# Expert blocks of a mixture layer: slots cut in quarters of 32, 21 units of work in place of 25, six weight tiles loaded ahead

## What is computed

```python
def _hier_moe(m, w_group, b_group, w_expert, b_expert, w_gate, w_up, w_down):
    ...
    g_w, g_idx = lax.top_k(g_prob, 1)              # one group of 4
    e_w, e_idx = lax.top_k(e_prob, MOE_TOP_K)      # two of its 8 experts
    ...
    def expert_block(args):
        tok, e = args
        xb = x_pad[tok]
        hb = jax.nn.silu(xb @ w_gate[e]) * (xb @ w_up[e])
        return hb @ w_down[e]
```

## Time and profile before

| what | value |
|---|---|
| median of three executions | 3107.17 us |
| profiled execution, first to last instruction (span) | 3105.2 us |
| PE busy | 94% of the span |
| DMA, mean | 199 GB/s |
| HBM read / written | 508.00 MB / 105.91 MB |

### The profile page before, as it was taken

One profiled execution on the slowest core, in us unless ns is written; L12 is line 12 of the kernel. 1 busy time (PEld: TensorE's weight loads), 2 busy tenths in 40 slices (PEclk: granted clock), 3 DMA queues, 4 the chain that ended last, 5 costly groups with the idle time before them and its releaser, 6 DMA issues. The chain is left out here.

```text
span 3105.2 us, 33224 instructions
## 1 busy us (share of the span) xinstructions
PE 2929.7 (94%) x12773; PEld 1588.7 (51%) x12774; DVE 1129.9 (36%) x2472; ACT 668.2 (22%) x1278; POOL 238.3 (8%) x344
## 2 busy tenths in 40 slices
PE   7999999999999999998989999878999999999898
PEld 4544555555644444434467744477655444444343
DVE  2585355544400000005464635565563000000152
ACT  3310355531110101003321124322211100101130
POOL 0000000001100000002000000143201000000110
PEclk9999999999999999998999999988999999999999
DMA  4000692031499999976020110000416999999731
GB/s 159 28 28 0 277 408 75 1 118 55 176 422 412 413 413 409 397 295 229 35 65 1 25 60 27 1 2 29 159 55 247 409 422 410 412 411 399 293 135 41
DMA packets 138552, 617.26 MB, mean 199 GB/s; under 512 B 25189, under 2 KB 31749, under 8 KB 121993
## 3 DMA queue, kind: packets, MB, share of 16 engines
q1 hardware_dynamic: 111848, 529.08, 43.1%
q0 software_dynamic: 23168, 82.85, 7.0%
q10 hardware_dynamic: 3376, 3.19, 0.3%
HBM read 508.00 MB, written 105.91 MB: 198 GB/s over the span
## 5 line engine op out<-in xcount | busy, mean ns | idle before, releaser
L1956 PE MATMUL acc<-wg,xt 128*128 128x512 f32 x512 | 223.7, 598 | 0.0
L2610 PE MATMUL acc<-xt,work 128*128 128x512 f32 x384 | 166.9, 593 | 0.0
L672 PE MATMUL acc<-h,xt 128*128 128x512 f32 x384 | 165.2, 592 | 0.0
L1956 PEld LDWEIGHTS acc<-wg,xt 128*128 128x128 f32 x512 | 97.8, 192 | 120.3 <-issue 120.3
L310 PE MATMUL scores<-qkt 65*128 65x512 f32 (+7 forms) x384 | 146.0, 489 | 0.4 <-DVE qkt L451 0.4
L457 DVE TENSOR_REDUCE nmax<-scores 128x1 f32<-128x256 f32 (+7 forms) x128 | 96.8, 756 | 74.0 <-PE scores L312 70.3
L1673 PE MATMUL py<-place 128*64 128x512 f32 (+1 forms) x352 | 121.9, 605 | 1.0 <-DVE place L1753 1.0
L1673 PE MATMUL pu<-place 128*128 128x512 f32 (+1 forms) x320 | 119.8, 593 | 0.0
L672 PEld LDWEIGHTS acc<-h,xt 128*128 128x128 f32 x384 | 72.9, 190 | 91.1 <-issue 90.9
L2610 PEld LDWEIGHTS acc<-xt,work 128*128 128x128 f32 x384 | 72.0, 190 | 86.1 <-issue 86.1
L1183 PE MATMUL acc<-place 128*128 128x512 f32 x256 | 112.7, 594 | 1.1 <-PEq L71 1.1
(11 more groups left out here) (647 smaller groups left out, 5195.6 us busy)
## 6 DMA issues: line engine op xcount, KB each, us to landing
own<-in_moe_w_gate_dram SPq DMA_DIRECT2D x22, 2048.0 KB, 18.8
place<-in_moe_w_down_dram SPq DMA_DIRECT2D x22, 2048.0 KB, 19.3
place<-in_moe_w_up_dram SPq DMA_DIRECT2D x20, 2048.0 KB, 19.8
slots_out<-zeros SPq DMA_DIRECT2D x4, 9216.0 KB, 62.9
place<-in_moe_w_gate_dram SPq DMA_DIRECT2D x18, 2048.0 KB, 23.3
own<-in_moe_w_up_dram SPq DMA_DIRECT2D x16, 2048.0 KB, 17.6
own<-in_moe_w_down_dram SPq DMA_DIRECT2D x10, 2048.0 KB, 22.3
xt<-in_moe_w_gate_dram SPq DMA_DIRECT2D x9, 2048.0 KB, 24.3
```

The source lines that it names most:

```text
L672: last = pe.matmul(acc[:, n % 4, 0:width], xs[:, k, tile_of(i)], weights[:, k, cols], start=(k == 0), stop=(k == k_of - 1))
L1956: last = pe.matmul(acc[:, u % 4, :], xt[:, k, i * P:(i + 1) * P], wg[:, k, n * SLAB:(n + 1) * SLAB], start=(k == 0), stop=(k == KD - 1))
L2610: last = pe.matmul(acc[:, n % 4, :], slabs[m // 4 % 2][:, k, (m % 4) * P:(m % 4 + 1) * P], xt[:, k, half * SLAB:(half + 1) * SLAB], start= ...
```

## The change

`expert_units` now makes units with parts of different sizes. Only two experts are fixed, with 128 slots each; the 16 heavy ranks have 96 slots, the 14 light ones 64 as before. Two heavy experts and one light one make two units (a trio): each unit has one heavy expert in rows 0 to 95 and 32 of the light one's 64 slots in rows 96 to 127. The six light experts left over make three pairs. That is 2 + 16 + 3 = 21 units. In a trio's unit each step of a product is three matmuls: the heavy expert's rows 0 to 63, its rows 64 to 95, and the light expert's rows 96 to 127.

A light expert's tiles are now read by two units. `weight_order` lays down a place for each tile by when it comes free, in place of n modulo 8. Six tiles are loaded ahead: experts 0 and 1, gate, up and down. `mixer_end` issues two of them as before, and four more when the mixer's last product is done, into memory that this product was the last to read. The rest of the arithmetic stays.

```diff
-HEAVY, FIXED, FIRST = 18, 3, 1e5
+HEAVY, FIXED, FIRST = 18, 2, 1e5
 RING = 8
+EARLY = 6
+QUAD = P // 4
...
+    heavies, lights = list(range(FIXED, HEAVY)), list(range(HEAVY, EXPERTS))
+    ranks, units = list(range(FIXED)), [[Part(q, 0, P)] for q in range(FIXED)]
+    trios, pairs = len(heavies) // 2, (len(lights) - len(heavies) // 2) // 2
+    assert 2 * trios == len(heavies) and trios + 2 * pairs == len(lights)
+    for n in range(trios):
+        q = len(ranks)
+        ranks += [heavies.pop(0), heavies.pop(0), lights.pop(0)]
+        units += [[Part(q, 0, 3 * QUAD), Part(q + 2, 3 * QUAD, QUAD)],
+                  [Part(q + 1, 0, 3 * QUAD), Part(q + 2, 3 * QUAD, QUAD, QUAD)]]
+        if pairs * (n + 1) // trios > pairs * n // trios:
+            q = len(ranks)
             ranks += [lights.pop(0), lights.pop(0)]
+            units.append([Part(q, 0, 2 * QUAD), Part(q + 1, 2 * QUAD, 2 * QUAD)])
...
+    free = {place: (-1, place) for place in range(RING)}
+    places = []
+    for kind, q in order:
+        place = min(free, key=free.get)
+        places.append(place)
+        free[place] = (3 * last[kind, q] + (1, 3, 5)[kind], 0)
+    return order, places, last
...
-                bring_in(nc, sp, own_loads, z["own_in"])
+                for n, (tile, view) in enumerate(own_loads):
+                    if n == 2:
+                        sp.wait_ge(z["products"], 2 * NT)
+                    sp.dma_start(tile, view).then_inc(z["own_in"], 16)
                 clear_used(sp)
...
-                step(dve.tensor_scalar(cap_col[:], rank[:], float(HEAVY), None, ALU.is_lt))
-                step(dve.tensor_scalar(cap_col[:], cap_col[:], float(P // 2), float(P // 2), ALU.mult, ALU.add))
+                step(dve.tensor_scalar(cap_col[:], rank[:], float(HEAVY), float(QUAD), ALU.is_lt, ALU.mult))
+                step(dve.tensor_scalar(position[:], rank[:], float(FIXED), float(QUAD), ALU.is_lt, ALU.mult))
+                step(dve.scalar_tensor_tensor(out=cap_col[:], in0=cap_col[:], scalar=float(2 * QUAD), in1=position[:], op0=ALU.add, op1=ALU.add))
...
-                    rows = P // len(units[n])
+                    cuts = (0, 2 * QUAD, 3 * QUAD, P)
+                    pieces = [(x.q, slice(max(a, x.row), min(b, x.row + x.rows))) for x in units[n] for a, b in zip(cuts, cuts[1:])
+                              if x.rows < P and a < x.row + x.rows and b > x.row] or [(units[n][0].q, slice(0, P))]
+                    if all(x.rows == 2 * QUAD for x in units[n]):
+                        pieces = [(x.q, slice(x.row, x.row + x.rows)) for x in units[n]]
                     for k in ks:
-                        for a, q in enumerate(units[n]):
-                            part = slice(a * rows, (a + 1) * rows)
+                        for q, part in pieces:
                             last = pe.matmul(out[part], lhs[:, k, part], weights_of(kind, q)[:, k, cols], start=(k == 0), stop=(k == k_last),
                                              skip_group_check=True)
...
-            ring = [own[:, n] for n in range(2)] + [x.rearrange("p a n -> p (a n)")[:, 0:KD * FF] for x in places]
...
-            places = [s5_t, gbz[:], xt[:, 0:4], xt[:, 4:8], gdn_t[:], work[:, 8:12]]
+            places = [s5_t, xt[:, 4:8], gdn_t[:], work[:, 8:12], gbz[:], xt[:, 0:4]]
...
-            moe(nc, c, t, layer, r, ch, ring, 2, m)
+            moe(nc, c, t, layer, r, ch, ring, EARLY, m)
```

More of the change, by code:

```diff
@@ L1050, with __init__, slots_of_rank @@
 ROUTES = GROUPS + EXPERTS
-HEAVY, FIXED, FIRST = 18, 3, 1e5
+HEAVY, FIXED, FIRST = 18, 2, 1e5
 RING = 8
-def expert_units():
[L1059 to L1067, removed]
+EARLY = 6
+QUAD = P // 4
+class Part:
+    def __init__(self, q, row, rows, slot=0):
+        self.q, self.row, self.rows, self.slot = q, row, rows, slot
+def expert_units():
+    heavies, lights = list(range(FIXED, HEAVY)), list(range(HEAVY, EXPERTS))
[9 more added lines that the diff above has]
+            q = len(ranks)
             ranks += [lights.pop(0), lights.pop(0)]
+            units.append([Part(q, 0, 2 * QUAD), Part(q + 1, 2 * QUAD, 2 * QUAD)])
     return ranks, units
+def slots_of_rank(rank):
+    return P if rank < FIXED else 3 * QUAD if rank < HEAVY else 2 * QUAD
 def weight_order(units):
-    order = []
+    order = [(kind, q) for q in range(FIXED) for kind in range(3)]
+    last = {}
     for n in range(len(units) + 1):
@@ L1077, in weight_order @@
             if 0 <= unit < len(units):
-                order += [(kind, unit, q) for q in units[unit]]
-    return order
+                for part in units[unit]:
+                    if (kind, part.q) not in order:
+                        order.append((kind, part.q))
+                    last[kind, part.q] = unit
+    free = {place: (-1, place) for place in range(RING)}
[5 more added lines that the diff above has]
+    return order, places, last
 class DeltaEnd:
@@ L1575, in first_blocks @@
     KF = FF // P
-    HALF = P // 2
     _, units = expert_units()
     UNITS = len(units)
-    tiles = weight_order(units)
-    at_tile = {(kind, q): n for n, (kind, _, q) in enumerate(tiles)}
+    tiles, places, last_user = weight_order(units)
+    at_tile = {tile: n for n, tile in enumerate(tiles)}
     arrivals = [sum(len(units[m]) for m in range(n % 2, n + 1, 2)) for n in range(UNITS)]
@@ L1600, in weights_of, with wait_weights @@
             def weights_of(kind, q):
[L1601 to L1606, removed]
+                return ring[places[at_tile[kind, q]]].rearrange("p (k n) -> p k n", k=KF if kind == 2 else KD)
+            def wait_weights(pe, kind, unit):
+                for part in units[unit]:
+                    n = at_tile[kind, part.q]
+                    if n >= preloaded:
+                        pe.wait_ge(tile_in[places[n]], 16 * places[preloaded:n + 1].count(places[n]))
             @block.sync
@@ L1809, in routing, with preloads @@
     return r
-def preloads(t, layer, own):
+def preloads(t, layer, ring):
     views = expert_weights(t, layer)
     _, units = expert_units()
-    return [(own[:, n].rearrange("p (k n) -> p k n", k=FF // P if kind == 2 else KD), views[kind][q])
-            for n, (kind, _, q) in enumerate(weight_order(units)[0:own.shape[1]])]
+    tiles, places, _ = weight_order(units)
+    return [(ring[places[n]].rearrange("p (k n) -> p k n", k=FF // P if kind == 2 else KD), views[kind][q])
+            for n, (kind, q) in enumerate(tiles[0:EARLY])]
 def moe(nc, c, t, layer, r, ch, ring, preloaded, m):
```

54 lines of the change are left out of this document (26 added, 28 removed).

## The result

The changed kernel takes 3808.49 us (median of three, 3800.95 to 3810.09) against 3107.17: 1.2239 times as long, interval 1.2212 to 1.2266. The forecast was 3051. What came is the rival *64 beside 32 doesn't overlap*, forecast at 3840 us with a chance of 0.14.

A forecast was written before the change was run, and what follows sets the result against it. PE and DMA were taken as nearly balanced, with DMA pacing after the change. Stages 28.9 and 26.9 us shorter (-56) and 0 for the rest took 3107.2 to about 3051 us; range 3014 to 3140 us, chance 0.8.

The forecast's parts named there:

- 64 beside 32 doesn't overlap: Rival on a trio's step: 2.00 us in place of 0.86, +367 us a layer, 3840 us in all; chance 0.14.
- PE's part: PE's time for the expert units: four units less and trios at a pair's cost, floor from 559 to 488 us a layer.
- The bound: Expert stage: PE and DMA nearly balanced, 559 and 540 us in layer 0; after the change DMA paces, 509.0 against 488.
- the bytes: DMA's load in a layer's expert stage after the change: 90 tiles and the units' rows, together 209.7 MB.
- DMA's slow start: Start of the expert stage: with fewer tiles issued at once, DMA loses 13 us and 2 us for first bytes, 15.
- waits of 2 to 5 us: PE's waits for weights in a unit of 22 us, which should leave its granted clock up.
- The rate: DMA in the expert stage: 412 GB/s for this mix of weights and rows, with bounds of 407 and 427.
- 538: Forecast length of a layer's expert stage in us: last tile landed at 524, then 14.3 for the last down product.
- The rest of the change: Early tiles in by about 822 us, extra row transfers hidden: 0; +5 us a layer if the last scatter queues.
- the second rival: The rival that 64 beside 32 doesn't overlap, 3840 us, chance 0.14; left outside the range.

The follow-up runs named there:

- E1: The changed kernel with a trio's step as four matmuls of 32 rows in place of 64, 32, 32; 3105.2 us, 0.9987 times the kernel before.
- E2: The changed kernel with all 64-row matmuls of a run first, then all its 32s; 3645.8 us, 1.1729 times the kernel before.
- E7: The kernel before with each pair's second expert as two matmuls of 32 rows in place of one of 64; 3482.1 us, ratio 1.1198.
- E5: E1 with a trio's rows moved as one transfer of 128 both in and out, in place of 96 and 32; 3060.4 us, ratio 0.9841.
- E9: E1 with only the rows going in to a trio's unit as one transfer of 128; 3066.5 us, 0.9863 times the kernel before.
- E3: The changed kernel with a trio's step as two matmuls of 64 rows; 3095.0 us, 0.9951 times the kernel before.
- E8: The kernel before with six weight tiles loaded ahead and the ring's places in another order; 3118.5 us, ratio 1.0022.

## Why the prediction was wrong

**The step that failed** is in *PE's part*: "I take 0.86: the nearest row is the pair's, the parts are on different columns, and their weight loads have no more columns together than a pair's." The step takes 2.00 us (1.98 by the weight loads). A matmul of 64 rows doesn't run beside one of 32, though two of 64 do and four of 32 do (E1). The forecast itself had the right other end, 2 x 0.86 + 2 x 0.14, read from the one row where rows 128 to 64 change shape. That row could have been read as a sign and not only as a price: if going to another shape costs time at all, two shapes may not be able to run together. That is an argument after the fact; what shows it are E1, E2 and E7. E7 shows that this step is enough for the loss, E1 that taking it away removes all of it. The Trainium skill's page "TensorEngine Tiling (Array Packing)", section "Tiling Modes", lists 128x64 and 128x32 as different modes and says that a change of mode drains TensorE. The traces agree: 0.12 to 0.14 us at each change, and no overlap across one. What the forecast set against it from the Trainium skill's page "TensorE: Matmul & The Clock Gate", section "Part 3: Packing small matmuls", pieces named by masks, doesn't carry over to matmuls of different width here.

**The size of the rival.** 3840 was forecast for it, 3808 came. +367 a layer was some 20 too much (346 and 348 came): 16 units at 21.93 + 27.39 us already hold the pair's 1.34 us, which the sum had added before (16 x 1.34 = 21).

**The bound.** That PE and DMA are nearly balanced, and that DMA would pace a faster PE, held in E1, E5 and E9: PE is busy 487.4 of 540.3 us in E1, where its floor was put at 488. So did the bytes: E1 moved 387 GB/s for 540.3 us, 209.1 MB, for 209.7 forecast. DMA's slow start was put at 15 us; E1's first three windows, against 397 GB/s, fall short by 2.8 + 8.1 + 3.3 = 14 us. That waits of 2 to 5 us would leave the granted clock up didn't quite hold: it was 0.94 in E1's middle.

**The rate** was mis-sized, and would have been also with a good shape: "412 GB/s is what this mix of weights and rows gets" holds where heavy experts' rows come 128 at a time (411 to 416 GB/s, with the pairs' 64 and 64 among them), not for 96 and 32 (397). 209.7 MB at 397 are 528 us for 509, and this is 19 of the 23 us by which E1's stage is longer than 538. The mix was taken as bytes, and its shapes changed with the change. This also answers for "POOL has four row transfers per trio's unit in place of two; [...] so they are hidden": POOL's own time is hidden, what they cost DMA is not.

**The rest of the change** was taken at 0, with +5 a layer kept. What it named as the danger, the last scatter queued behind a tile, is what the trace looks like: the scatter landed late while early tiles were moving, and the rows' fetch came 4.9 us later (829.52 for 824.62). PE's first turn started 2.6 us later, and the first gate product took 2.8 us more at the lower clock: it ended 5.4 us later, near the +5. That DMA would be done by 822 us was wrong, its share is 1.01 up to 826. The early tiles pay only where DMA paces, 13 us.

**The range**, 3014 to 3140, left out the second rival, which was the one that came. E1 would have been inside it, at "no change", and with a rate that the range had no room for (397 GB/s for its 407 to 427).

## What to carry to other kernels

In these runs column tiles (matmuls that fill different columns of TensorE) ran side by side only when they had the same width. So cut all parts into the narrowest width: four of 32 cost no more than two of 64, 22.55 and 22.58 us for a trio's unit in E1 and E3. Don't put 64 beside 32 in one step, and where widths must follow each other, sort them: each change costs 0.13 us. When a change packs work more tightly, look at the shape of its transfers as well as at their bytes: where DMA paces, a transfer of 96 partitions cost more than one of 128. Large loads issued ahead of a small transfer on which TensorE waits make it late, and where the granted clock is already low, it can come back later behind that wait, so that the loss is near twice the wait.

## What the runs showed of the hardware

- Shapes in one product: two of 64 rows, 0.43 us a pass; four of 32, 0.43 to 0.45; 64 and two 32s, 1.98 to 2.00 us for a step of two passes, where equal widths take 0.86: 4 x 0.43 one after the other, and two changes of shape of 0.12 to 0.14.
- The busy share of DMA doesn't tell a rate that can be had. In E8 it is 1.00 over 485 us at 392 GB/s while PE is never idle, in the kernel before 1.01 at 412, in E1 1.02 at 397 while PE is idle 14% of the time. E8's window:

```profile
855.00:1340.00 485.00, 485.00 (x1549) 213.36 (x1547) 44.86 (x65) 48.80 (x66) 28.87 (x54) 1.00 1.00 392
```

- After 2.35 us of waiting at the stage's start, behind a stretch with the granted clock at 0.60, 16 matmuls took 9.85 us (clock 0.69 and then 0.74 in 6 us each). In the kernel before, behind a stretch at 0.50 but with a wait of only 0.30 us, the same 16 took 7.13 (0.98 and 1.00).
- Rows into the chip's memory as 96 and 32 lowered the rate from 414 to 397 GB/s; results out of it in the same pieces didn't.
